# First two modulation items between the turns of x, sum of squares behind them, cached rows ahead of the key items

## The chip, the cores and the metric

The kernel runs on one core of a Trainium2 chip. The metric is the device time of one execution in microseconds (us); lower is better.

## The reference

One decoder layer (DEPTH = 1) is computed for a prompt of 256 tokens and for 8 sequences that each decode one token behind 1024 cached positions, in fp32, with D = 1024. Reduced to what matters here:

```python
mod = silu(c) @ ada_w + ada_b              # 9 rows of c (1 prompt, 8 samples), ada_w 1024 x 6144
sh1, sc1, g1, sh2, sc2, g2 = split(mod, 6)
h = rms_norm(x, norm1_w) * (1 + sc1) + sh1  # needs the first third of mod: sh1, sc1
proj = h @ w_in                             # 1024 x 2824: pool, q, k, v, conv q/k/v, z, b, a
q_a, k_a = rms_norm per head                # block-sparse attention, paged K/V cache for the samples
qkv = silu(short_conv(concat(state_conv, [q_d, k_d, v_d])))   # width 4, 3 cached rows per sample
beta, g = gates from b, a;  o = gated_delta_rule(l2norm(q), l2norm(k), v, g, beta, state)
x = x + g1 * (concat(pool, attention, delta) @ w_out)
x = x + g2 * ((silu(h2 @ w_gate) * (h2 @ w_up)) @ w_down)   # h2 = rms_norm(x) modulated by sh2, sc2
```

`rms_norm` divides by the root of the mean of squares over the 1024 channels of a token.

## The kernel before

The kernel is written engine by engine, with semaphores by hand. Tokens lie in the free dimension: `xT`, `hT` and `proj` are [128 channels, chunks, 264 tokens], 256 prompt tokens and the 8 samples. All weights and all cached pages come through a ring of five slots of 1 MB, filled by SyncE (SP) in the order of the list `stream` (L75 to L114); a slot is filled again when the item five places before it has been read. The stream begins with the eight 1 MB blocks of `ada_w` that make sh1 and sc1. Two blocks make one modulation item: `ada(j)` (L346) multiplies blocks 2j and 2j+1 by the turned silu of c (`cT`), and `ada_turn(j)` (L368) turns the result back after ScalarE has copied it (`ada_rows`, L1530). VectorE adds it up in `mod_reduce(j)` (L948), and `norm_half` (L966) applies it to `hT`.

Before the items TensorE turns x and c (L379 to L388) and the small constant rows (L391), and adds the squares that ScalarE makes of each chunk of x over the channels (`ss1`, L392). ScalarE takes the root of that sum (`roots`, L1547), VectorE its reciprocal and multiplies x with it into `hT` (L945, L946). `keep_awake(b, n)` (L338) issues n matmuls of the identity into bank b, which compute nothing that is used; it waits until the bank is free. At the same time GpSimd (POOL) makes masks (L1792 to L1833) and then issues ten small transfers: cached pool and convolution states, the eight gate columns of `w_in` (`wba`), constants, and two copies of states (L1834 to L1850).

Behind that, the list `ORDER` (L86) sets for all engines alike the order of the steps: each engine walks it and does its own part of a step. W1 is a block of two 128-column groups of `w_in` (`project`, L411). QSUM, QNORM and QR make the query norms and the query rows, which POOL stores and spreads over the partitions (L1859 to L1863) for the key items: K0 to K15 are half-sequences of cached keys, each a product and a reduction on VectorE (`k_item`, L1010). CONV is the short convolution on VectorE (`convolve`, L1119), which needs the projections up to W9 and the cached rows; BA and AB make the gates; DSUM and DNORM the norms of its q and k. CEXT stands for the cached rows. On TensorE it is

```python
def cached_rows():
    pe.wait_ge(sem("cst_in"), 16)
    b = opened("cext", 3)
    ... six transposes of cst
    closed(last, "cext")
    pe.wait_ge(sem("pool_rows"), 1)
    b = opened("pdT8", 3)
    ... two transposes of pd8
    closed(last, "pdT8")
```

`opened(name, b)` waits until the last contents of bank b were read, here until VectorE's part of CEXT (L1098) has copied `cext`. That part copies `cext`, waits for `pdT8` and copies that.

Of the kernel before, what the change touches and what calls it, by code (L numbers as in the profile page):

```python
# [35 lines left out]
def build(nc, x_prompt, x_sample, cache_k, cache_v, state_pool, state_conv, state_delta, page_table,  # L36
# [4 lines left out]
    _, T, D = x_prompt.shape  # L41
# [11 lines left out]
    DC = D // P  # L53
# [18 lines left out]
    IW = SLOT // DC  # L72
# [10 lines left out]

    ORDER = ("W1 W2 QSUM W7 QNORM QR QB0 QB1 K0 W8 K1 K2 W9 CEXT W10 CONV BA AB W3 DSUM QB2 K3 W4 DNORM KSUM K4 GN W5 "  # L86
             "QB3 K5 GC KNORM GBC KR ROWS KK W6 K6 QB4 TI VR L1 K7 KROW W0 K8 M1 VROW L2 QB5 K9 M2 TAILS L3 S K10 M3 A4 "
             "H0 QB6 K11 L4 M4 H1 A5 H2 L5 K12 M5 A6 QB7 H3 K13 H4 L6 K14 M6 POOL H5 UA A7 K15 H6 UB UC H7 UD A8 HE OWN "
             "A9 DMAX DEXP V0 XA V1 XB V2 XC V3 XD V4 MX V5 V6 MW0 V7 VE MD MW1").split()
    ORDER = [(st.rstrip("0123456789"), int("0" + st.lstrip("ABCDEFGHIJKLMNOPQRSTUVWXYZ"))) for st in ORDER]  # L90
    for st, n in ORDER:
        if st == "W":
# [7 lines left out]

    win_order = [n for st, n in ORDER if st == "W"]

# [16 lines left out]
    with ctx:  # L119
# [6 lines left out]
        def sem(name):  # L126
            if name not in sems:
                sems[name] = ctx.enter_context(nc.semaphore(name))
            return sems[name]
# [143 lines left out]

        EARLY = sum(st == "MW" for st, n in ORDER)
        part_free = {}
# [12 lines left out]
        def full(eng, name):  # L288

            b, n = filled[name]  # L290
            eng.wait_ge(bank_full[b], n)
            return bank[b]

        def freed(ins, name):
            ins.then_inc(bank_free[filled[name][0]], 1)
# [24 lines left out]
        def _(pe):  # L320
            def opened(name, b, readers=1):

                if frees[b]:
                    pe.wait_ge(bank_free[b], frees[b])
                fills[b] += 1
                frees[b] += readers
                assert name not in filled, name
                filled[name] = (b, fills[b])
                freed_by[name] = frees[b]
                return bank[b]  # L330

            def closed(ins, name):
                ins.then_inc(bank_full[filled[name][0]], 1)
# [4 lines left out]
            def keep_awake(b, n):  # L338

                if n and frees[b]:  # L340
                    pe.wait_ge(bank_free[b], frees[b])
                for _ in range(n):
                    mm(bank[b][:, 0:P], ident[:, :], ident[:, :])


            def ada(j, b_=3, awake=0):  # L346

                opened(f"ada{j}", b_)
                for n in range(2):
                    keep_awake(1, awake)  # L350
                    last = ada_half(j, n)
                    if n == 0:
                        used_up(last, ("ada", 2 * j), "pe_read")
                closed(last, f"ada{j}")
                read_by(f"ada{j}", ("ada", 2 * j + 1))
# [20 lines left out]
            pe.wait_ge(sem("ident_made"), 1)  # L376
            keep_awake(7, 8)
            pe.wait_ge(sem("x_in"), 16 * (TT + 1))
            for c in range(DC):  # L379
                b = opened(f"xT{c}", 4 + c % 4)  # L380
                for r in range(TT):
                    pe.transpose(b[:, r * P:(r + 1) * P], x_nat[:, r, c * P:(c + 1) * P], ident[:, :])  # L382
                closed(pe.transpose(b[:, T:NT], x_nat[0:NS, TT, c * P:(c + 1) * P], ident[0:NS, 0:NS]), f"xT{c}")
            pe.wait_ge(sem("c_silu"), 1)
            b = opened("cT", 0)
            for c in range(DC):
                last = pe.transpose(b[:, c * NC:(c + 1) * NC], c_nat[:, c * P:(c + 1) * P], ident[32:32 + NC, 32:32 + NC])
            closed(last, "cT")  # L388
            pe.wait_ge(sem("rows_in"), 16 * 11)
            b = opened("rowsT", 1)  # L390
            closed(pe.transpose(b[:, 0:NR], rows[0:NR, :], ident[0:NR, 0:NR]), "rowsT")  # L391
            b = opened("ss1", 6)  # L392
            for c in range(DC):
                pe.wait_ge(sem("sq1"), c + 1)
                last = mm(b[:, 0:NT], ones[:, :], hT[:, c, :], c == 0, c == DC - 1)
            closed(last, "ss1")
            pe.wait_ge(sem("cT_made"), 1)
            ada(0, 2)
            ada(1, 3)
            ada_turn(0, 0)  # L400
            ada(2, 2)
            ada_turn(1, 1)
            keep_awake(0, 4)
            ada(3, 3, 2)
            ada_turn(2, 0)
            keep_awake(1, 3)
            ada_turn(3, 1)
            keep_awake(0, 8)
            pe.wait_ge(sem("masks_made"), 1)
# [390 lines left out]
            }  # L800
            for st, n in ORDER:
                if st in go:
# [28 lines left out]
            for i in range(D // IW):  # L831
                w = parts(("wout", i))
                for n in range(2):
                    j = 2 * i + n
# [77 lines left out]
        def _(v):  # L912
# [16 lines left out]
            for c in range(PCH):  # L929
                for g in range(2):  # L930
                    r = slice(64 * g, 64 * g + 64)
                    step(v.tensor_scalar(rcnt[r, c, :], rcnt[r, c, :], float(WINDOWS[2 * c + g]), None, ALU.min))
            for c in range(DC):
                b = full(v, f"xT{c}")
                freed(v.tensor_copy(xT[:, c, :], b[:, 0:NT]), f"xT{c}")
            b = full(v, "cT")
            freed(v.tensor_copy(cT[:, :, 0:NC], b[:, 0:DC * NC].rearrange("p (c r) -> p c r", c=DC)), "cT")
            v.wait_ge(bank_free[0], frees_at("cT"))
            v.sem_inc(sem("cT_made"), 1)
            b = full(v, "rowsT")  # L940
            freed(v.tensor_copy(constT[:, 0:NR], b[:, 0:NR]), "rowsT")
            v.wait_ge(bank_free[1], frees_at("rowsT"))
# [565 lines left out]
        def _(a):  # L1508
# [29 lines left out]
            def roots(name, banks, scale, done):  # L1538
                for c in range(banks):
                    nm = f"{name}{c}" if banks > 1 else name  # L1540
                    b = full(a, nm)
                    freed(a.activation(rbc[:, c, :], b[:, 0:NT], ACT.Sqrt, bias=eps[:, 0:1], scale=scale), nm)
                    a.wait_ge(bank_free[filled[nm][0]], frees_at(nm))
                    a.sem_inc(sem(done), 1)


            roots("ss1", 1, 1.0 / D, "root1")  # L1547
            for j in range(2 * D // IW // 2):
                ada_rows(j)

            def proj_out(item):
# [385 lines left out]
        @block.sync  # L1937
        def _(sp):
            sp.dma_start(c_nat[0:1, :], c_prompt).then_inc(sem("c_in"), 16)
            sp.dma_start(c_nat[1:NC, :], c_sample).then_inc(sem("c_in"), 16)  # L1940
            cols = {"ada": ada_w, "win": w_in, "wout": w_out, "gate": w_gate, "up": w_up}
            for it in stream:
                kind, i = it
                if it == ("k", (0, 0)):
                    sp.wait_ge(sem("table_in"), 16)
                if kind in "kv":

                    load_pages(sp, it, range(PGI // 2 if kind == "v" and i[0] >= 2 else PGI))
                    continue
                if it in before:  # L1950
                    sp.wait_ge(*released[before[it]])
                s = place[it][0]
                dst = ring[:, s, :]
                if kind == "down":
                    k0, k1 = DKT[i[1]]
                    sp.dma_start(dst[:, 0:(k1 - k0) * IW].rearrange("p (k n) -> p k n", n=IW),
                                 w_down[0, k0 * P:k1 * P].rearrange("(k p) n -> p k n", p=P)[:, :, i[0] * IW:(i[0] + 1) * IW])\
                      .then_inc(slot_full[s], 16)
                else:
                    sp.dma_start(dst.rearrange("p (k n) -> p k n", k=DC),  # L1960
                                 cols[kind][0].rearrange("(k p) n -> p k n", p=P)[:, :, i * IW:(i + 1) * IW])\
                      .then_inc(slot_full[s], 16)
                if it == ("win", 6):

                    sp.wait_ge(sem("sq1"), 1)
                    for c in range(GC):
                        for w in range(2):
                            sp.dma_start(Ss[64 * w:64 * w + 64, :, c, :],
                                         state_delta[0, :, 2 * c + w].rearrange("q k n -> k q n")).then_inc(sem("S_in"), 16)

            rows_at = 0
            for i in range(D // IW):
                cols_i = slice(i * IW, (i + 1) * IW)
                for r in (0, 2, 1) if i == D // IW - 1 else range(TT + 1):
                    if (i, r) == (D // IW - 1, 1):
                        sp.wait_ge(sem("y_last"), 1)
                    else:
                        rows_at += 1
                        sp.wait_ge(sem("y_rows"), rows_at)
                    if r < TT:  # L1980
                        sp.dma_start(y_prompt[0, r * P:(r + 1) * P, cols_i], ynat[:, r, cols_i]).then_inc(sem("y_out"), 16)
                    else:
                        sp.dma_start(y_sample[:, 0, cols_i], ynat[0:NS, TT, cols_i]).then_inc(sem("y_out"), 16)
            sp.wait_ge(sem("y_out"), 16 * (TT + 1) * (D // IW))
# [29 lines left out]
```

## Time and profile before

| what | value |
|---|---|
| median of 3 runs | 596.73 us (593.17 to 600.68) |
| the profiled execution | 596.88 us |
| its span, first to last instruction | 594.9 us |
| TensorE busy | 534.4 us, 90% of the span |
| VectorE busy | 350.0 us, 59% |
| ScalarE busy | 163.5 us, 27% |
| moved by DMA | 116.79 MB, mean 196 GB/s |
| mean granted TensorE clock | 0.947 of full speed |

A busy TensorE counts matmuls from start to modelled end, so its 90% is not 90% of its peak, and keep-awake matmuls are in it. The granted clock has two levels, 1.2 and 2.4 GHz; 1.00 in a row is the higher, 0.50 the lower, and a value between is a mean over the stretch. The chain of work that ended last says which instruction or transfer each next one waited for, back from the end. In a timeline row the bracket gives how long the engine stood idle before and what it waited for.

### The profile page before, as it was taken

To read this page: it belongs to the slowest core of one execution; us is meant where nothing else is said; L and a number is where in the kernel's file an instruction comes from. 1 tells how busy PE (TensorE), PEld (TensorE's weight loads), DVE (VectorE), ACT (ScalarE), POOL (GpSimd) and SP (SyncE) were. 2 spreads that over 40 slices of the span, in tenths; PEclk is the share of its full clock that TensorE was granted. 3 is DMA by queue.
4 is the path that set the end of the run, shared out by engine and by line. 5 is a ranking of instruction groups with operands and counts; after the bars stand their busy time and mean duration, and the time that the engine had idled before them with its cause. 6 is when DMAs were issued, how large, how long until landed. Compare 5 with 4: busy or idle time off the path is not lost.

```text
span 594.9 us, 10233 instructions
## 1 busy us (share of the span) xinstructions
PE 534.4 (90%) x3943; PEld 450.2 (76%) x3943; DVE 350.0 (59%) x548; ACT 163.5 (27%) x230; POOL 56.6 (10%) x126
## 2 busy tenths in 40 slices
PE   7879997997998888988789689987999999999997
PEld 5557775675688766865564059887999999999996
DVE  4540269478798787955734537465665566455441
ACT  4101010811132122211000224364343443424420
POOL 6800010000104800000101000000000000000000
PEclk8979897997699999999969899998999999999999
DMA  9996356476049467643739998595465655645201
GB/s 294 332 302 207 108 189 218 123 204 221 19 150 324 144 221 245 217 132 119 244 111 376 384 352 268 173 298 163 148 209 162 195 169 168 195 144 193 73 19 37
DMA packets 98998, 116.79 MB, mean 196 GB/s; under 512 B 6317, under 2 KB 81278, under 8 KB 98934
## 3 DMA queue, kind: packets, MB, share of 16 engines
q1 hardware_dynamic: 93218, 104.42, 54.8%
q10 hardware_dynamic: 3908, 7.42, 3.5%
q0 software_dynamic: 1824, 4.30, 2.6%
q8 instruction: 31, 0.51, 0.4%
q14 instruction: 17, 0.14, 0.1%
HBM read 113.30 MB, written 2.99 MB: 195 GB/s over the span
## 4 chain that ended last, share of the span: by engine, by line
PE 64%; DVE 21%; DMA 7%; ACT 3%; issue 3%; ACTq 1%; SPq 0%; DVEq 0%
PE bank L336 61%; DVE prod L916 5%; DVE s_all L1019 5%; DVE mats L916 3%; DMA ring<-in_ada_w_dram 2%; DMA ring<-in_w_out_dram 2%; DVE BTP L916 1%; DVE cv L1127 1%; DMA ring<-in_cache_v_dram 1%; DMA x_nat<-in_x_sample_dram 1%; PE bank L373 1%; PE bank L382 1%; ACT w_part L1692 1%; DMA qb<-q_rows_dram 1%; PE bank L517 1%
## 5 line engine op out<-in xcount | busy, mean ns | idle before, releaser
L336 PE MATMUL bank<-a_hi,w_part 128*128 128x264 f32 x832 | 153.5, 286 | 2.1 <-DVE a_lo L1464 2.1
L916 DVE TENSOR_TENSOR w_part<-ring,w_part 128x2048 fp32r<-128x2048 f32 (+1 forms) x38 | 84.9, 2236 | 89.2 <-ACT w_part L1692 89.2
L336 PEld LDWEIGHTS bank<-a_hi,w_part 128*128 128x128 f32 x832 | 129.8, 189 | 2.6 <-issue 2.6
L336 PE MATMUL bank<-a_lo,w_part 128*128 128x264 f32 x416 | 118.4, 285 | 0.0
L1692 ACT ACTIVATE w_part<-ring 128x2048 fp32r<-128x2048 f32 (+1 forms) x38 | 70.9, 1871 | 86.0 <-PE bank L336 75.0
L336 PE MATMUL bank<-hT,ring 128*128 128x264 f32 x352 | 85.7, 406 | 0.8 <-ACT proj L1555 0.8
L336 PEld LDWEIGHTS bank<-hT,ring 128*128 128x128 f32 x352 | 70.0, 201 | 14.9 <-issue 2.4
L336 PEld LDWEIGHTS bank<-a_lo,w_part 128*128 128x128 f32 x416 | 79.0, 190 | 0.1
L336 PE MATMUL bank<-hid_hi,w_part 128*128 128x264 f32 x352 | 64.9, 285 | 0.0
L336 PEld LDWEIGHTS bank<-ident 128*128 128x128 f32 x362 | 48.1, 212 | 10.4 <-issue 5.6
L336 PEld LDWEIGHTS bank<-hid_hi,w_part 128*128 128x128 f32 x352 | 54.5, 188 | 0.1
L336 PE MATMUL bank<-ident 128*128 128x128 f32 x362 | 51.5, 301 | 3.3 <-POOLq L1785 1.9
L336 PE MATMUL bank<-hid_lo,w_part 128*128 128x264 f32 x176 | 49.7, 282 | 0.0
L916 DVE TENSOR_TENSOR prod<-ring,qb 128x2048 f32<-128x2048 f32 x16 | 36.5, 2280 | 7.0 <-DMA qb<-q_rows_dram 6.4
L1019 DVE TENSOR_REDUCE s_all<-prod 128x32 f32<-128x2048 f32 x16 | 36.6, 2286 | 0.5
L1555 ACT ACTIVATE proj<-bank 128x264 f32<-128x264 f32 x22 | 8.6, 390 | 89.5 <-PE bank L336 89.4
L336 PEld LDWEIGHTS bank<-hid_lo,w_part 128*128 128x128 f32 x176 | 33.2, 188 | 0.0
L336 PE MATMUL bank<-ring,cT 128*32 128x256 f32 x384 | 24.3, 393 | 6.0 <-DMA ring<-in_ada_w_dram 6.0
L336 PE MATMUL bank<-mats,BTP 128*128 128x128 f32 x192 | 25.0, 280 | 3.4 <-DVEq L1085 2.9
L336 PEld LDWEIGHTS bank<-mats,BTP 128*128 128x128 f32 x192 | 22.9, 191 | 5.2 <-issue 4.0
L336 PE MATMUL bank<-ring,prod 128*32 128x512 f32 x128 | 18.0, 660 | 6.5 <-DMA ring<-in_cache_v_dram 6.5
L336 PEld LDWEIGHTS bank<-ring,cT 128*32 128x32 f32 x384 | 11.3, 111 | 15.3 <-DMA ring<-in_ada_w_dram 6.9
(326 smaller groups left out, 570.3 us busy)
## 6 DMA issues: line engine op xcount, KB each, us to landing
ring<-in_ada_w_dram SPq DMA_DIRECT2D x24, 1024.0 KB, 7.3
ring<-in_cache_k_dram SPq DMA_DIRECT2D x64, 256.0 KB, 3.6
ring<-in_w_in_dram SPq DMA_DIRECT2D x11, 1024.0 KB, 5.6
ring<-in_w_gate_dram SPq DMA_DIRECT2D x11, 1024.0 KB, 5.3
ring<-in_w_up_dram SPq DMA_DIRECT2D x11, 1024.0 KB, 5.3
ring<-in_cache_v_dram SPq DMA_DIRECT2D x40, 256.0 KB, 4.2
ring<-in_w_down_dram SPq DMA_DIRECT2D x8, 1024.0 KB, 5.1
ring<-in_cache_v_dram ACTq DMA_DIRECT2D x24, 256.0 KB, 5.2
```

What stands on the lines that cost most here:

```text
L336: return pe.matmul(out, lhsT, rhs, start=start, stop=stop, skip_group_check=True)
L373: last = pe.transpose(b[:, n * P:(n + 1) * P], ada_flat(j)[:, n * P:(n + 1) * P], ident[:, :])
L382: pe.transpose(b[:, r * P:(r + 1) * P], x_nat[:, r, c * P:(c + 1) * P], ident[:, :])
L517: last = pe.transpose(b[:, n * P:(n + 1) * P], sm[:, h % 2, n * P:(n + 1) * P], ident[:, :])
L916: return v.tensor_tensor(out, a, b_, op)
L1019: ins = v.tensor_reduce(s_all[:, o:o + PGI * H], prod[:, :].rearrange("p (g d) -> p g d", d=HD), AX, ALU.add)
L1127: v.scalar_tensor_tensor(out=cv[:, c, back:T], in0=proj[:, CV0 + c, 0:T - back], scalar=cw(i, c), in1=cv[:, c, back:T], op0=ALU.mult, op1= ...
L1555: freed(a.activation(proj[:, j, :], b[:, 0:NT], ACT.Copy), f"proj{j}")
L1692: inc(a.activation(w_hi[:, n % PARTS, 0:c], arrived(a, item)[:, 0:c], ACT.Copy), "w_high")
```

## The change

In TensorE's first part, c is turned after four of the eight chunks of x instead of after all. The first modulation item is multiplied right behind the turns, then the constant rows are turned, the second item is multiplied, and the sum of squares follows. Two of four keep-awake matmuls ahead of the fourth item and three between the last two turns are taken out. VectorE takes the turned chunks in the same order, and ScalarE copies the first item ahead of the root. In `ORDER`, CEXT moves from behind W9 to behind QSUM, for all engines. SyncE's wait ahead of the delta states' loads, which overwrite the rows of x, is for all eight squares.

```diff
@@ -83,7 +83,7 @@
 
 
 
-    ORDER = ("W1 W2 QSUM W7 QNORM QR QB0 QB1 K0 W8 K1 K2 W9 CEXT W10 CONV BA AB W3 DSUM QB2 K3 W4 DNORM KSUM K4 GN W5 "
+    ORDER = ("W1 W2 QSUM CEXT W7 QNORM QR QB0 QB1 K0 W8 K1 K2 W9 W10 CONV BA AB W3 DSUM QB2 K3 W4 DNORM KSUM K4 GN W5 "
              "QB3 K5 GC KNORM GBC KR ROWS KK W6 K6 QB4 TI VR L1 K7 KROW W0 K8 M1 VROW L2 QB5 K9 M2 TAILS L3 S K10 M3 A4 "
              "H0 QB6 K11 L4 M4 H1 A5 H2 L5 K12 M5 A6 QB7 H3 K13 H4 L6 K14 M6 POOL H5 UA A7 K15 H6 UB UC H7 UD A8 HE OWN "
              "A9 DMAX DEXP V0 XA V1 XB V2 XC V3 XD V4 MX V5 V6 MW0 V7 VE MD MW1").split()
@@ -376,34 +376,39 @@
             pe.wait_ge(sem("ident_made"), 1)
             keep_awake(7, 8)
             pe.wait_ge(sem("x_in"), 16 * (TT + 1))
-            for c in range(DC):
+            def turn_x(c):
+
                 b = opened(f"xT{c}", 4 + c % 4)
                 for r in range(TT):
                     pe.transpose(b[:, r * P:(r + 1) * P], x_nat[:, r, c * P:(c + 1) * P], ident[:, :])
                 closed(pe.transpose(b[:, T:NT], x_nat[0:NS, TT, c * P:(c + 1) * P], ident[0:NS, 0:NS]), f"xT{c}")
+
+            for c in range(DC // 2):
+                turn_x(c)
             pe.wait_ge(sem("c_silu"), 1)
             b = opened("cT", 0)
             for c in range(DC):
                 last = pe.transpose(b[:, c * NC:(c + 1) * NC], c_nat[:, c * P:(c + 1) * P], ident[32:32 + NC, 32:32 + NC])
             closed(last, "cT")
+            for c in range(DC // 2, DC):
+                turn_x(c)
+            pe.wait_ge(sem("cT_made"), 1)
+            ada(0, 2)
             pe.wait_ge(sem("rows_in"), 16 * 11)
             b = opened("rowsT", 1)
             closed(pe.transpose(b[:, 0:NR], rows[0:NR, :], ident[0:NR, 0:NR]), "rowsT")
+            ada(1, 3)
             b = opened("ss1", 6)
             for c in range(DC):
                 pe.wait_ge(sem("sq1"), c + 1)
                 last = mm(b[:, 0:NT], ones[:, :], hT[:, c, :], c == 0, c == DC - 1)
             closed(last, "ss1")
-            pe.wait_ge(sem("cT_made"), 1)
-            ada(0, 2)
-            ada(1, 3)
             ada_turn(0, 0)
             ada(2, 2)
             ada_turn(1, 1)
-            keep_awake(0, 4)
+            keep_awake(0, 2)
             ada(3, 3, 2)
             ada_turn(2, 0)
-            keep_awake(1, 3)
             ada_turn(3, 1)
             keep_awake(0, 8)
             pe.wait_ge(sem("masks_made"), 1)
@@ -930,13 +935,19 @@
                 for g in range(2):
                     r = slice(64 * g, 64 * g + 64)
                     step(v.tensor_scalar(rcnt[r, c, :], rcnt[r, c, :], float(WINDOWS[2 * c + g]), None, ALU.min))
-            for c in range(DC):
+            def take_x(c):
+
                 b = full(v, f"xT{c}")
                 freed(v.tensor_copy(xT[:, c, :], b[:, 0:NT]), f"xT{c}")
+
+            for c in range(DC // 2):
+                take_x(c)
             b = full(v, "cT")
             freed(v.tensor_copy(cT[:, :, 0:NC], b[:, 0:DC * NC].rearrange("p (c r) -> p c r", c=DC)), "cT")
             v.wait_ge(bank_free[0], frees_at("cT"))
             v.sem_inc(sem("cT_made"), 1)
+            for c in range(DC // 2, DC):
+                take_x(c)
             b = full(v, "rowsT")
             freed(v.tensor_copy(constT[:, 0:NR], b[:, 0:NR]), "rowsT")
             v.wait_ge(bank_free[1], frees_at("rowsT"))
@@ -1544,8 +1555,9 @@
                     a.sem_inc(sem(done), 1)
 
 
+            ada_rows(0)
             roots("ss1", 1, 1.0 / D, "root1")
-            for j in range(2 * D // IW // 2):
+            for j in range(1, 2 * D // IW // 2):
                 ada_rows(j)
 
             def proj_out(item):
@@ -1962,7 +1974,7 @@
                       .then_inc(slot_full[s], 16)
                 if it == ("win", 6):
 
-                    sp.wait_ge(sem("sq1"), 1)
+                    sp.wait_ge(sem("sq1"), DC)
                     for c in range(GC):
                         for w in range(2):
                             sp.dma_start(Ss[64 * w:64 * w + 64, :, c, :],
```

## Rows read from the trace of the kernel before

**Rows 1.** Chain that ended last, first 72 us: start us, us, what.

```profile
22.05 12.68 DMA ring<-in_ada_w_dram
...
37.76 1.28 PE bank L336 x6
...
39.89 16.32 PE bank L336 x80
```

**Rows 2.** Stretches: us, engines' busy us (count), PEclk, DMA share, GB/s.

```profile
8.00:20.00 12.00, 12.00 (x71) 8.38 (x74) 7.83 (x12) 5.59 (x11) 8.92 (x37) 0.72 1.10 348
20.00:22.00 2.00, 2.00 (x44) 1.21 (x40) 1.97 (x2) 0.60 (x1) 1.68 (x6) 1.00 0.80 233
22.00:29.00 7.00, 5.23 (x68) 3.22 (x60) 2.67 (x5) 1.20 (x2) 6.28 (x10) 1.00 1.10 365
29.00:34.00 5.00, 1.53 (x20) 0.78 (x12) 0.00 (x0) 0.00 (x0) 1.92 (x4) 0.95 1.05 172
```

**Rows 3.** Timeline, first 45 us: start, us, engine, line, operation, [idle before].

```profile
7.37 1.06 ACT L1525 ACTIVATE x_nat<-x_nat 9x1024 f32<-9x1024 f32 x1
...
12.65 1.01 PE L387 MATMUL bank<-ident,x_nat 9*128 9x9 f32 x8
...
18.80 3.66 PE L336 MATMUL bank<-ring,cT 128*32 128x256 f32 x64
...
21.31 2.36 DVE L916 TENSOR_TENSOR hT<-xT,rbc 128x2112 f32<-128x2112 f32 x1
21.35 2.41 POOL L1829 TENSOR_SCALAR_AFFINE_SELECT lvl<-lvl 128x64 f32<-128x64 f32 x1
...
24.72 0.57 POOL L1834 DMA_DIRECT2D mats<-in_state_pool_dram  x1 [0.65 <-POOL lvl L1831]
...
37.86 0.60 ACT L1534 ACTIVATE adaS<-bank 128x512 f32<-128x512 f32 x1 [10.02 <-PE bank L373]
```

**Rows 4.** Timeline of SyncE, 19 to 23 us: sixth to eighth block.

```profile
19.93 2.70 SPq L1960 DMA_DIRECT2D ring<-in_ada_w_dram  x3
```

**Rows 5.** Timeline, 59 to 98 us: W7, reciprocal, query norm, CEXT, W10, convolution.

```profile
59.77 7.39 PE L336 MATMUL bank<-hT,ring 128*128 128x264 f32 x32
...
60.42 1.79 DVE L991 RECIPROCAL rbc<-rbc 8x264 f32<-8x264 f32 x1 [14.44 <-ACTq L1597]
...
67.83 0.93 DVE L997 SCALAR_TENSOR_TENSOR proj<-proj,constT,bank 128x264 f32<-128x264 f32 x2 [5.62 <-PE bank L336]
...
92.85 0.31 DVE L1100 COPY cext<-bank 128x144 f32<-128x144 f32 x1
...
93.30 0.35 PE L476 MATMUL bank<-ident,vb 8*128 8x8 f32 x2 [5.42 <-DVE cext L1100]
...
93.58 9.73 PE L336 MATMUL bank<-hT,ring 128*128 128x264 f32 x32
...
93.97 1.69 DVE L1122 TENSOR_SCALAR cv<-proj,constT 128x264 f32<-128x264 f32 x6
```

**Rows 6.** Timeline, 103 to 128 us: gates, W3, squares, DSUM, W4, DNORM.

```profile
103.25 3.73 PE L336 MATMUL bank<-hT,wba 128*4 128x264 f32 x32
...
106.91 7.39 PE L336 MATMUL bank<-hT,ring 128*128 128x264 f32 x32
...
107.74 1.08 ACT L1618 ACTIVATE mats<-cv 128x1056 f32<-128x1056 f32 x1
...
114.23 1.95 PE L336 MATMUL bank<-mats,headsum 128*8 128x264 f32 x8
...
116.94 7.36 PE L336 MATMUL bank<-hT,ring 128*128 128x264 f32 x32 [0.77 <-ACT proj L1555]
...
127.28 1.69 DVE L1154 SCALAR_TENSOR_TENSOR cv<-cv,bank 128x264 f32<-128x264 f32 x4 [1.74 <-PE bank L336]
```

**Rows 7.** Stretches at a lower granted clock; columns as in rows 2.

```profile
71.50:74.80 3.30, 3.30 (x11) 2.62 (x10) 0.68 (x1) 0.00 (x0) 0.52 (x1) 0.55 0.06 15
...
93.30:103.10 9.80, 9.80 (x34) 7.90 (x34) 9.20 (x34) 0.39 (x1) 0.00 (x0) 0.74 0.51 180
```

## Prediction

> **What bounds the kernel.** I read four things in turn: the chain that ended last over the first 72 us, the stretches of that part with their DMA share, the timeline around each moved step, and the granted clock behind each long wait of TensorE. In the chain, TensorE is through with its first work by 22 us and then the chain is one transfer for 12.68 us: the eighth modulation block, the last of `ada_w` that the first norm needs, landing at 34.7 [rows 1]. From 39.89 on it is TensorE's dense work, and behind that TensorE and VectorE alternate, so a shift of the chain at 40 us or at 94 us goes through to the end. I see no later transfer that waits for a fixed time: the value pages too wait for ring slots, which work on the chain frees. In the stretches the reader is to see that the DMA engines are full from 8 us to 34 us except for two microseconds: 348 GB/s, then 233, then 365, then 172 although the share is 1.05 [rows 2].
>
> **The front, and what it can gain.** Turns of x run from 7.5 us. The silu of c ends at 8.43 (7.37 + 1.06), before the fourth turn is over, so `cT` between the turns makes nobody wait; its eight transposes (1.01 us) only change places [rows 3]. The matmuls of `ada(0)` then start at about 13.9 instead of 18.80 (18.80 less the sum of squares, which moves behind). The first block is read by about 15.7, so the sixth to eighth blocks are queued at 15.7 to 19 instead of from 19.93 on [rows 4]. What this buys is only the hole that they left in the queue: (348 - 233) GB/s x 2 us is 230 KB, or 0.7 us at 348 GB/s [rows 2]. Beyond that the blocks cannot come faster than 348 GB/s.
>
> Then comes the stretch from 29 to 34 us at 172 GB/s [rows 2]. It is the one in which POOL's own transfers (cached states, `wba`, `poolw`), issued from 24.72 on, are in flight [rows 3]. POOL gets to them after its masks, and one mask instruction took 2.41 us beside VectorE's 2.36 us product of x and the root, where its neighbours take some 0.24 [rows 3]. That product needs the sum of squares, which now ends near 23.4 (the second item is through near 19.8, when its fourth block has landed; then 16 matmuls, half of W3's 7.39 [rows 6]), so it runs at some 26 to 28 us: POOL issues about 2.2 us earlier, still ahead of the eighth block. So I take it that the slow stretch stays in front of the eighth block, and count 0.7. The ends: 0 if the earlier POOL transfers cost the blocks as much as the hole did, and 0.7 + (348 - 172) / 348 x 5 us = 3.2 if the slow stretch falls behind the block. I take 0.7 because nothing in the rows moves POOL's transfers later.
>
> The Trainium skill, "DMA: Bandwidth & Descriptors", section on queues, rings and completion order, says that a DMA engine goes round between the queues that have work, a packet of each at a time. By it POOL's earlier start takes turns from the blocks, and the front would give nothing; the 172 GB/s agrees, but no row shows the order of the packets.
>
> The later sum of squares costs nothing: before, the product ended 4.9 us after the sum (21.31 + 2.36 less 18.80), so now near 28.3, and the first two reductions by about 29.3, under cover of the eighth block until about 34. If that block landed before 29, they would be next. `keep_awake(0, 2)` waits for bank 0, freed by the first of these reductions at about 28.5; behind it only the seventh block's matmuls are queued, which ran near that time anyway. Of the keep-awake matmuls taken out, those of 1.28 us between the last two turns were on the chain [rows 1], but the last turn also waits for ScalarE's copy (37.86 + 0.60) [rows 3]: I take 0.2, ends 0 and 1.28. SyncE's wait for eight squares instead of one, far into the stream, is fulfilled long before: 0. No DMA changes its place on SyncE's queue, since CEXT loads nothing. Front: 0.9 us earlier.
>
> **CEXT ahead of W7.** On TensorE it opens bank 3 twice; the second opening (`pdT8`) waits until VectorE has copied the first. Where it stands now that copy waits behind three key items, and TensorE waits 5.42 us [rows 5]. That wait is off the chain: the convolution behind it needs W9 only, done before. In its new place VectorE still has the query reciprocal ahead of the copy (60.42 + 1.79 = 62.21). Copy to second transpose is 93.30 - 92.85 = 0.45, and from there to the next weights 93.58 - 93.30 = 0.28 [rows 5]. So W7 starts at 62.98 by the old clock instead of 59.77: 3.2 us late. VectorE hides nothing of it: it stood 5.62 us idle for W7 and the query spread [rows 5]. Queued behind W7 are the spread, the query rows, their two transfers, and K0 to K2: all 3.2 us later. On VectorE the two copies and their handshakes vanish from between K2 and the convolution: 93.97 - 92.85 = 1.1 back [rows 5]. Their new cost lies in VectorE's idle 5.62. Net, the convolution starts 2.1 late.
>
> **What is late next.** With the wait gone, TensorE runs W10 (7.4 at full rate, as W3), the gates (3.73) and W3 (7.39) straight behind W9, and is through with W3 near 108.7 (the old end of W9 at 87.9, + 3.2 - 0.9, and these three) instead of 114.2. Nobody can use this. DSUM needs the squares that ScalarE ends at 107.74 + 1.08 = 108.8 [rows 6], now later by 2.1 - 0.9 = 1.2, so at 110.0; it takes 1.95. W4 needs banks that ScalarE frees after its decay work, at 116.94, now 118.1 [rows 6]. VectorE's decay step no longer waits for the gates, but ScalarE is the late one there: 0. So TensorE stands idle from about 112.0 to 118.1, 6 us where it was 0.77 [rows 6]. The only wait of that length nearby is the 5.42 before W10; there the granted clock went to the lower level, 1.2 GHz, for part of the stretch (mean 0.74), and W10 took 9.73 us against 7.39 for the same work [rows 5 to 7]. W4 I expect to take the same 2.3 us more. This is on the chain: VectorE idles 1.74 for the spread behind W4 [rows 6]. Ends: 0 (clock held) and 7.4 (all of W4 at half rate); I stay at the one row for such a wait.
>
> **The sum.** - 0.9 + 3.2 - 1.1 + 2.3 = +3.5 us on the profiled execution's 596.88 (span 594.9 and 2.0 around it): 600.4. The median shown, 596.73, is 0.15 below that execution, so against it 600.2. The three runs spread over 593.17 to 600.68, so 2% (12 us) is about what can be told from no change, and the forecast is "no change", on the slow side.
>
> **Rivals.** W7 runs at the lower clock too. TensorE now idles some 2.3 us before it. For: after smaller gaps near 70 us the clock went down for 71.5 to 74.8 (mean 0.55), costing 0.45 x 3.3 = 1.5 us [rows 7]. Against: the wait of 0.77 before W4 cost nothing. Sum +5.0: 601.7.
>
> The front gives nothing, by POOL's transfers coming 2.2 us earlier. For: the 172 GB/s. Against: the hole at 20 to 22 us is certain. Only the 0.2 is left: +4.2, 600.9. This is also what the Trainium skill's rule gives.
>
> W4 keeps its clock. Then +1.2: 597.9. Against it stands the only wait of like length.
>
> Faster. The slow stretch falls behind the eighth block: front 3.2 + 0.2, and with all shifted W4 at full rate: -3.4 + 2.1 = -1.3, 595.4. It decides where the eighth block lands before 32 us. Against: POOL issues earlier, not later.
>
> Slower beyond 2%. VectorE's later alternation with TensorE holds key items between steps of the triangular solve at fixed places. If the shift sent TensorE to the lower clock there, as before W10, at 2.3 us each four such places on top of the sum pass 12 us (3.5 + 9.2 = 12.7): 609.4. Nothing in the change moves the order there, so I count it little.
>
> **How the numbers follow.** Chances: forecast 0.38, W7 also slow 0.20, no front gain 0.16, W4 keeps its clock 0.10, faster 0.12, slower beyond 0.04. All but the last lie within 2%: faster 0.01 (a front and a clock better than both ends), same 0.95, slower 0.04. The range goes from the faster case, 595.4, less a little for the spread of the runs, to W7 slow and no front together (+3.5 + 1.5 + 0.7 = +5.7: 602.4), with as much on top for a longer stretch at the lower clock in W4: 595 to 604.
>
> **What would show it.** After: `ada(0)` near 14 us; the hole at 20 to 22 us gone; the eighth block near 34.0; a wait of TensorE for VectorE's `cext` copy of 2 to 2.5 us, now at about 60 to 62 us; K0's product 2.3 us later than before; no wait before W10; TensorE idle about 6 us before W4, and W4 near 9.7 us. I am wrong if the eighth block lands before 32, if W7 starts no later than before, or if W4 takes 7.4.

## The result, and the profile after

The changed kernel takes 602.53 us (median of 12 runs, 601.09 to 609.22), the kernel before, run beside it, 599.23 us (12 runs). The ratio is 1.0087 with a 95% interval of 1.0048 to 1.0126: slower by some 5.2 us (2.9 to 7.5), under 2% but clear of noise. The ratio compares the means of the fast runs (603.7 and 598.5 us, one slow run of the kernel before left out), while the medians lie 3.3 us apart. The profiled execution took 601.52 us with a span of 599.6 us, 4.7 us more than before.

The chain of waits of the changed kernel (start us, us, what; answers to [rows 1]):

```profile
19.84 15.43 DMA ring<-in_ada_w_dram
...
39.75 16.04 PE bank L336 x80
```

Its stretches (columns as in [rows 2]):

```profile
8.00:20.00 12.00, 12.00 (x89) 6.79 (x93) 4.85 (x11) 5.48 (x11) 8.92 (x37) 1.00 1.10 348
20.00:22.00 2.00, 2.00 (x18) 1.38 (x11) 2.00 (x1) 0.61 (x1) 1.43 (x7) 1.00 1.10 349
22.00:26.80 4.80, 4.80 (x49) 3.32 (x48) 2.26 (x2) 1.08 (x2) 4.33 (x8) 1.00 1.14 357
26.80:34.30 7.50, 3.47 (x32) 2.22 (x31) 3.36 (x5) 0.60 (x1) 1.85 (x4) 1.00 1.08 238
```

The reader is to see that the hole at 20 to 22 us is closed (349 GB/s for 233), that the slow stretch has come forward and grown longer, and that the transfer on the chain ends at 35.3 (34.7 before), while x landed 0.5 us later. The 1.00 granted from 8 to 20 us, for 0.72 before, is not to be read as a gain. Two transposes of x take 0.69 us there, as they did before once the clock had fallen (0.50 from 10 to 12 us), and not the 0.44 of the higher clock. The first line is of the changed kernel, the two others of the kernel before:

```profile
8.00 0.69 PE L383 MATMUL bank<-ident,x_nat 128*128 128x128 f32 x2 [2.31 <-DMA x_nat<-in_x_sample_dram]
...
7.49 0.44 PE L382 MATMUL bank<-ident,x_nat 128*128 128x128 f32 x2 [1.79 <-DMA x_nat<-in_x_sample_dram]
...
9.58 0.68 PE L382 MATMUL bank<-ident,x_nat 128*128 128x128 f32 x2
```

Its timeline up to W1 (start us, us, engine, line, operation; answers to [rows 3, 4]):

```profile
9.83 12.58 SPq L1972 DMA_DIRECT2D ring<-in_ada_w_dram  x4
...
15.31 3.23 PE L336 MATMUL bank<-ring,cT 128*32 128x256 f32 x32
...
22.48 0.57 POOL L1846 DMA_DIRECT2D mats<-in_state_pool_dram  x1 [0.65 <-POOL lvl L1843]
...
26.83 2.36 DVE L921 TENSOR_TENSOR hT<-xT,rbc 128x2112 f32<-128x2112 f32 x1
...
35.31 1.94 PE L336 MATMUL bank<-ring,cT 128*32 128x256 f32 x16 [2.74 <-DMA ring<-in_ada_w_dram]
...
39.09 0.66 PE L373 MATMUL bank<-ident,adaS 128*128 128x128 f32 x4 [0.80 <-ACTq L1547]
```

The steps come in the forecast order, and POOL issues 2.24 us earlier (22.48 for 24.72), as forecast. `ada(0)` starts at 15.31 instead of near 14, and the eighth block, at 35.31, is no earlier. The last turn now runs at the higher clock (0.66 us); before, it took 1.06:

```profile
38.83 1.06 PE L373 MATMUL bank<-ident,adaS 128*128 128x128 f32 x4
```

What two queues moved from the start of the span to the landing of the eighth block (packets, MB, share of the 16 engines; q1 is SyncE's queue, q0 POOL's), first before, to 34.73 us, then after, to 35.27 us:

```profile
q1 hardware_dynamic: 8739, 8.84, 85.9%
q0 software_dynamic: 271, 0.28, 4.8%
...
q1 hardware_dynamic: 9016, 9.11, 87.0%
q0 software_dynamic: 384, 0.46, 6.6%
```

After, 0.18 MB more of POOL's transfers and 0.27 MB more of SyncE's queue, that is of the blocks behind the eighth, were moved by the time the eighth had landed.

From QSUM to the convolution (answers to [rows 5]):

```profile
59.99 1.79 DVE L1002 RECIPROCAL rbc<-rbc 8x264 f32<-8x264 f32 x1 [13.47 <-ACTq L1609]
61.71 0.23 DVE L1111 COPY cext<-bank 128x144 f32<-128x144 f32 x1
...
62.09 0.26 PE L481 MATMUL bank<-ident,vb 8*128 8x8 f32 x2 [2.21 <-DVE cext L1111]
...
62.27 9.07 PE L336 MATMUL bank<-hT,ring 128*128 128x264 f32 x32
...
72.10 0.89 DVE L1008 SCALAR_TENSOR_TENSOR proj<-proj,constT,bank 128x264 f32<-128x264 f32 x2 [9.48 <-PE bank L336]
...
90.42 7.39 PE L336 MATMUL bank<-hT,ring 128*128 128x264 f32 x32 [0.43 <-DMA ring<-in_w_in_dram]
...
96.65 1.69 DVE L1133 TENSOR_SCALAR cv<-proj,constT 128x264 f32<-128x264 f32 x6
```

The 5.42 us that TensorE waited for the copy before W10 have become 2.21 before W7; W10 is at full rate (7.39), but W7 takes 9.07 where it took 7.39. The clock behind that wait, as a stretch (answers to [rows 7]):

```profile
62.00:66.00 4.00, 3.91 (x11) 3.15 (x12) 0.17 (x1) 0.00 (x0) 0.00 (x0) 0.57 0.02 4
```

From W3 to DNORM (answers to [rows 6]):

```profile
101.40 7.39 PE L336 MATMUL bank<-hT,ring 128*128 128x264 f32 x32
...
111.54 1.95 PE L336 MATMUL bank<-mats,headsum 128*8 128x264 f32 x8 [2.76 <-ACT mats L1630]
...
119.61 9.43 PE L336 MATMUL bank<-hT,ring 128*128 128x264 f32 x32 [6.12 <-ACT proj L1567]
...
132.01 1.70 DVE L1165 SCALAR_TENSOR_TENSOR cv<-cv,bank 128x264 f32<-128x264 f32 x4 [3.85 <-PE bank L336]
```

TensorE has W3 behind it 5.5 us sooner and then idles 6.12 us before W4, which takes 9.43 for 7.36. The clock at the start of W4, as a stretch:

```profile
119.61:123.50 3.89, 3.89 (x9) 3.06 (x10) 1.59 (x1) 2.11 (x3) 0.00 (x0) 0.50 0.00 0
```

To compare executions whose x lands at different times I take distances in each trace: from the first turn of x to the eighth block's first matmul, from there to W1, and from W1's start to later starts (with the duration in brackets). K4 is the key item behind W4; "rest" is from K4 to the end of the span. The rows below "after" are the experiments of the next section.

| kernel | x to block 8 | block 8 to W1 | W7 | K0 | convolution | W4 | K4 | rest |
|---|---|---|---|---|---|---|---|---|
| before | 27.29 | 7.01 | 17.98 (7.39) | 37.12 | 52.18 | 75.15 (7.36) | 90.90 | 462.2 |
| after | 27.31 | 6.06 | 20.90 (9.07) | 41.34 | 55.28 | 78.24 (9.43) | 96.06 | 462.2 |
| a2_again | 27.89 | 8.10 | 21.26 (8.95) | 41.41 | 55.35 | 78.31 (9.42) | 96.12 | 465.3 |
| e1_front | 27.46 | 8.11 | 18.44 (7.39) | 38.35 | 53.41 | 76.45 (7.36) | 92.19 | 463.5 |
| e2_cext | 29.94 | 4.74 | 20.90 (7.39) | 39.28 | 53.23 | 76.19 (9.73) | 94.30 | 462.6 |
| e3_bank5 | 28.33 | 4.73 | 18.57 (7.39) | 37.31 | 51.25 | 74.20 (9.73) | 92.32 | 464.7 |
| e4_awake | 28.46 | 4.74 | 22.88 (7.39) | 41.49 | 55.43 | 84.33 (7.29) | 100.00 | 464.6 |
| e5_awake_fit | 27.51 | 6.06 | 20.90 (7.39) | 40.51 | 54.46 | 77.76 (7.29) | 93.43 | 462.0 |
| e6_bank5_awake | 28.49 | 8.10 | 19.00 (7.39) | 37.72 | 51.66 | 76.30 (7.29) | 91.97 | 460.3 |
| p1_pool_only | 25.34 | 4.74 | 17.96 (7.39) | 37.20 | 52.26 | 75.22 (7.36) | 90.96 | 462.8 |
| p2_front_pool | 25.20 | 4.74 | 17.97 (7.39) | 37.77 | 52.82 | 75.78 (7.36) | 91.53 | 463.2 |
| p3_all | 24.71 | 4.73 | 18.57 (7.39) | 37.15 | 51.10 | 74.05 (7.36) | 89.80 | 461.1 |
| p4_behind_qr | 24.61 | 4.73 | 17.98 (7.39) | 37.09 | 51.04 | 73.99 (7.36) | 89.73 | 462.7 |
| p5_no_awake | 24.62 | 4.73 | 17.97 (7.39) | 38.03 | 51.97 | 74.93 (9.22) | 92.53 | 462.5 |

So after less before is: W1 0.42 earlier (41.37 for 41.79), W7 2.92 later and 1.68 longer, the way from W7's end to K0 0.38 shorter, from K0 to the convolution 1.12 shorter, W4 2.07 longer, the rest equal: 4.7 us. W1 itself is 0.93 earlier against x, and x landed 0.51 later.

### The profile page after: what moved, and what is told of

Its sections match the earlier page's. It is cut to its first block, busy times and chain, and to the rows that moved or that the text cites. A ratio compares the mean times of both kernels' runs of the same rounds, so it can differ in the third digit from the quotient of the medians.

```text
span 599.6 us, 10213 instructions
## 1 busy us (share of the span) xinstructions
PE 532.8 (89%) x3933; PEld 447.4 (75%) x3933; DVE 349.6 (58%) x548; ACT 163.3 (27%) x230; POOL 54.3 (9%) x126
## 4 chain that ended last, share of the span: by engine, by line
PE 64%; DVE 21%; DMA 7%; ACT 3%; issue 3%; ACTq 1%; DVEq 0%
PE bank L336 60%; DVE prod L921 5%; DVE s_all L1030 5%; DMA ring<-in_ada_w_dram 3%; DVE mats L921 3%; DMA ring<-in_w_out_dram 2%; DVE BTP L921 1%; DVE cv L1138 1%; DMA ring<-in_cache_v_dram 1%; DMA x_nat<-in_x_sample_dram 1%; PE bank L383 1%; PE bank L373 1%; ACT w_part L1704 1%; DMA qb<-q_rows_dram 1%; PE bank L522 0%
## 5 line engine op out<-in xcount | busy, mean ns | idle before, releaser
L336 PEld LDWEIGHTS bank<-ident 128*128 128x128 f32 x352 | 45.7, 208 | 12.5 <-issue 5.1
L336 PE MATMUL bank<-ident 128*128 128x128 f32 x352 | 49.4, 298 | 5.6 <-DVE modT L963 2.3
L336 PE MATMUL bank<-ring,cT 128*32 128x256 f32 x384 | 25.6, 409 | 2.7 <-DMA ring<-in_ada_w_dram 2.7
```

What stands on the lines that cost most here:

```text
L336: return pe.matmul(out, lhsT, rhs, start=start, stop=stop, skip_group_check=True)
```

## Experiments

Each diff is against the changed kernel unless it says otherwise. Where a run has a ratio, it is to the kernel before, run beside it, and need not be the quotient of the two medians; a single profiled execution stands behind each line of the table.

**The front alone.**

```diff
-"W1 W2 QSUM CEXT W7 QNORM ... K2 W9 W10 ..."
+"W1 W2 QSUM W7 QNORM ... K2 W9 CEXT W10 ..."
```

> The changed kernel with CEXT back behind W9, so only the part up to W1. Theory (the whole loss comes from CEXT, the front is a small gain): W1 starts 0.4 to 1 us earlier than before against the landing of x, and the time is 0 to 1 us under the kernel before, ratio 0.998 to 1.000. Within it: the eighth block lands no earlier (27.3 us behind the landing of x, as in both kernels so far), and the gain is the keep-awake matmuls left out. Rival (the sum of squares behind the two items is late and costs): W1 later, ratio above 1.003.

Measured: 0.997 (0.9932 to 1.0007), 597.79 us. The eighth block lies 27.46 us behind x, as expected, so it gains nothing. In the profiled execution, which at 602.41 us was the second longest of twelve, W1 is not earlier: it comes 8.11 us behind the block, at the lower clock, where eleven of the other executions have 4.7 to 7.0 and two have 8.10. A small gain is likely and not shown; a loss as large as the change's is excluded.

**CEXT alone**, in the kernel before.

```diff
-"W1 W2 QSUM W7 QNORM ... K2 W9 CEXT W10 ..."
+"W1 W2 QSUM CEXT W7 QNORM ... K2 W9 W10 ..."
```

> The kernel before with only CEXT moved ahead of W7. Theory: W7 starts 2.5 to 3.2 us late, runs at the lower clock at first (about 1.7 more), the convolution starts about 3.7 late, TensorE idles 6 us before W4 and W4 takes 2 us more; the key item behind it is 5 to 6 us late, ratio 1.009 to 1.011. Rival (the wait is covered, the loss is in the front): ratio 0.998 to 1.002.

Measured: 1.0084 (1.0051 to 1.0117), 603.48 us: as slow as the whole change. The lines of its timeline:

```profile
63.27 0.26 PE L476 MATMUL bank<-ident,vb 8*128 8x8 f32 x2 [2.21 <-DVE cext L1100]
63.45 7.39 PE L336 MATMUL bank<-hT,ring 128*128 128x264 f32 x32
...
118.74 9.73 PE L336 MATMUL bank<-hT,ring 128*128 128x264 f32 x32 [4.84 <-ACT proj L1555]
```

The wait is the same 2.21 us, yet W7 kept the full clock in this execution. K4 lies 3.40 us later against W1 than before (94.30 for 90.90): this is the case that I had forecast as the likeliest, with 4.4 for these terms. My expectation of a slow W7 here was a miss, though this execution (601.40 us) was the fastest of its twelve, and it does not tell how W7 ran in the others.

**CEXT without the wait.**

```diff
-b = opened("pdT8", 3)                        # TensorE
+b = opened("pdT8", 5)
-v.wait_ge(bank_free[3], frees_at("pdT8"))    # VectorE
+v.wait_ge(bank_free[5], frees_at("pdT8"))
```

> The changed kernel with the second transpose group of CEXT (pdT8) in bank 5 instead of bank 3, so that TensorE does not wait for VectorE's copy. Theory: W7 starts 0.5 us behind QSUM's end at the full clock (7.4 us), K0 is on time, the convolution starts about 2 us earlier than before, but TensorE still idles some 6 us before W4, which takes 9.4 us: the two cancel, ratio 0.998 to 1.002. If W4's clock is not on the chain: 2 us faster than before, ratio 0.996. If the wait at W7 is not what costs: as the changed kernel, ratio 1.008.

Measured: 1.0028 (0.9997 to 1.006), 599.11 us; its interval ends below the changed kernel's 1.0087, but overlaps that kernel's interval, which begins at 1.0048. So the time leans to a gain over the changed kernel and does not settle it.

```profile
58.45 0.27 PE L481 MATMUL bank<-ident,vb 8*128 8x8 f32 x2
58.65 7.39 PE L336 MATMUL bank<-hT,ring 128*128 128x264 f32 x32
...
114.28 9.73 PE L336 MATMUL bank<-hT,ring 128*128 128x264 f32 x32 [4.83 <-ACT proj L1567]
```

No wait, W7 0.59 later than before against W1, the convolution 0.93 earlier; and still K4 is 1.42 later, because W4 has the lower clock. The gain of moving CEXT is eaten there.

**Keep-awake matmuls in both waits**, first too many.

```diff
 closed(last, "cext")
+keep_awake(4, 18)          # e5_awake_fit: 9
 ...
+if item == 4:
+    keep_awake(3, 48)      # e5_awake_fit: 22
```

> The changed kernel with keep-awake matmuls in its two new waits: 18 between CEXT's two transpose groups, 48 ahead of W4. The waits stay as long. Theory (wait 2.5 net of the front, W7's clock 1.7, W4's clock 2.1): W7 and W4 at 7.4 us each, the time about 3.8 us under the changed kernel, ratio to the kernel before 1.001 to 1.003. Rival (the clock is off the chain, only the wait counts): as the changed kernel, ratio 1.008.

Measured: 1.0087 (1.0049 to 1.0125), 606.04 us. I had taken 0.12 us for one keep-awake matmul; in the trace it is 0.23 to 0.24:

```profile
113.92 10.98 PE L336 MATMUL bank<-ident 128*128 128x128 f32 x96
124.74 7.29 PE L336 MATMUL bank<-hT,ring 128*128 128x264 f32 x32
```

48 of them (96 instructions) took 11.0 us, so W7 and W4 were pushed later by the filler. The run says nothing on the question, and was repeated with half.

> The changed kernel with keep-awake matmuls that fit its two new waits: 9 (2.2 us at 0.244 each, as the trace shows) between CEXT's transpose groups, 22 (5.4 us) ahead of W4; the run before had twice that and pushed W7 and W4 later itself. Theory (the clock at W7 and W4 is on the chain): W7 and W4 at 7.4 us, W4's start as in the changed kernel, the key item behind it 2 to 4 us nearer to W1 than there (96.06 us behind W1's start), ratio to the kernel before 1.002 to 1.005. Rival (only the wait counts): 96 us behind W1, ratio 1.008.

Measured: 1.0017 (0.9974 to 1.0059), 601.74 us. The interval overlaps the changed kernel's, so the trace has to decide.

```profile
62.23 7.39 PE L336 MATMUL bank<-hT,ring 128*128 128x264 f32 x32
...
114.08 5.18 PE L336 MATMUL bank<-ident 128*128 128x128 f32 x44
119.09 7.29 PE L336 MATMUL bank<-hT,ring 128*128 128x264 f32 x32
```

W7 starts exactly as in the changed kernel against W1 (20.90) and takes 7.39; W4 takes 7.29; K4 is 2.63 nearer to W1 (93.43 for 96.06). That work which computes nothing shortens the way to K4 shows that the clock after the two waits is on the chain. What is left against before is 2.53 us: the wait at W7 (2.92), 0.47 between W7 and K0, where the clock fell somewhat later instead (0.50 from 74 to 76 us), and 0.33 at W4's start, which the fill pushed; off this come 1.11 for the copies taken from VectorE and 0.08 behind W4's start.

**No wait and a filled idle time.** Bank 5 as above, and 22 keep-awake matmuls ahead of W4.

> CEXT ahead of W7 with pdT8 in bank 5 (no wait) and 22 keep-awake matmuls ahead of W4. Theory: W7 0.6 us later than before against W1, the convolution 0.9 earlier, W4 0.9 earlier and at the full clock, so the key item behind it 0.9 earlier against W1 (90.0 instead of 90.9); with the front, ratio 0.995 to 0.998. Rival (W4's clock off the chain): as the run with bank 5 alone, 92.3 behind W1, ratio 1.003.

Measured: 0.9982 (0.9948 to 1.0017), 598.43 us. W4 at 7.29. In this execution the lower clock still held behind W1's start (W1 and W2 took 14.84 for 14.41), and the fill pushed W4 (its keep-awake matmuls took 6.30 us, part of them at the lower clock), so K4 lies at 91.97 and not at 90.0. Against before no more than "not slower" is shown. Against the changed kernel a gain is shown, since the two intervals lie apart: without the wait, and with the idle time filled, the loss is gone.

**POOL's transfers behind the eighth block**, with the front alone and with the kernel before.

```diff
+g.wait_ge(sem("ada_rows"), 4)
 g.dma_start(pbuf, state_pool[0]...)
```

> The front of the change alone (CEXT behind W9) with POOL's ten transfers issued only after ScalarE's fourth copy, that is behind the eighth block. Theory (the front gained nothing at the eighth block because POOL's transfers, earlier by 2.2 us, took the DMA engines that the closed hole gave): the slow stretch moves behind the block, which lands 3 us earlier, some 24.3 us behind the landing of x instead of 27.3, W1 2 to 3 us earlier, ratio 0.991 to 0.995. Rival (the block is late for another reason, as its own queue): 27.3 us, ratio as the front alone, 0.997.

Measured: 0.9889 (0.9845 to 0.9934), 593.51 us. Its stretch from 29 to 34 us, and its timeline:

```profile
29.00:34.00 5.00, 4.58 (x48) 2.82 (x48) 1.01 (x4) 0.00 (x0) 0.00 (x0) 1.00 1.10 349
```

```profile
29.36 1.35 PE L336 MATMUL bank<-ident 128*128 128x128 f32 x8 [2.08 <-DVE modT L963]
30.64 1.07 PE L336 MATMUL bank<-ring,cT 128*32 128x256 f32 x16
31.64 0.71 PE L336 MATMUL bank<-ident 128*128 128x128 f32 x4
32.28 1.07 PE L336 MATMUL bank<-ring,cT 128*32 128x256 f32 x16
```

The stretch that stood at 172 GB/s is at 349. The eighth block's matmuls start 2.1 us earlier behind x (25.20 for 27.29), not the 3 expected, and no longer wait for it: TensorE waits 2.08 us for `modT` ahead of `keep_awake(0, 2)`, which is the late sum of squares coming through VectorE. TensorE no longer stands idle ahead of the block (2.74 us in the changed kernel, 4.25 before), and the clock stays up: block 8 to W1 4.74 for 6.06 and 7.01.

> The kernel before with only POOL's ten transfers issued behind ScalarE's fourth copy (order of the front and CEXT as before). It tells what the hole of 2 us in the DMA engines is worth once nothing else is ahead of the eighth block. Theory (hole 0.7 us, POOL's transfers the rest): the eighth block lands some 26 us behind the landing of x, against 25.2 with the changed front and 27.3 before; ratio 0.990 to 0.994. Rival (the changed front is what lets the late transfers gain): 27.3, ratio 0.998 or more.

Measured: 0.9939 (0.9907 to 0.9971), 592.95 us.

```profile
20.00:22.00 2.00, 2.00 (x40) 1.20 (x40) 1.46 (x1) 0.59 (x2) 1.42 (x7) 1.00 0.45 141
22.00:29.00 7.00, 5.83 (x83) 3.61 (x72) 3.71 (x6) 1.67 (x3) 0.00 (x0) 1.00 1.03 329
29.00:34.00 5.00, 3.70 (x45) 2.15 (x44) 0.00 (x0) 0.00 (x0) 0.00 (x0) 1.00 1.10 349
```

With the old front the block lies 25.34 us behind x, with the hole wide open (141 GB/s). The two fronts differ by 0.14 us here, and by 0.63 to 0.73 against the three runs below, which have the new front too (24.61 to 24.71). Each front has its own brake: the old one the hole, the new one the late sum of squares. What the closed hole is worth by itself stays open.

**All together, and CEXT where VectorE waits anyway.** p3_all: the change with bank 5, 22 keep-awake matmuls ahead of W4 and POOL late. p4_behind_qr: the same with CEXT behind QR. p5_no_awake: that without the keep-awake matmuls.

```diff
-"W1 W2 QSUM CEXT W7 QNORM QR QB0 ..."
+"W1 W2 QSUM W7 QNORM QR CEXT QB0 ..."
```

> All together: the change with pdT8 in bank 5, 22 keep-awake matmuls ahead of W4, and POOL's transfers behind the eighth block. Theory: the gains add, W1 about 24.3 + 5 us behind the landing of x, the key item behind W4 90 us behind W1, ratio 0.988 to 0.993. Rival (late POOL transfers hold up W1's or W2's weights or the cached rows): no faster than the front alone, 0.997.

Measured: 0.9892 (0.9847 to 0.9937), 592.5 us of 6 runs; K4 89.80 behind W1.

> The changed front, POOL's transfers late, CEXT behind QR (where VectorE waits 6 us for the query rows) with pdT8 in bank 5, and 22 keep-awake matmuls ahead of W4. Theory: W7 as before (17.98 us behind W1's start), the convolution 1.1 earlier, W4 1.1 earlier at the full clock, the key item behind W4 some 89.5 to 89.8 us behind W1 (before 90.9); ratio 0.985 to 0.990. Rival: W4's start does not follow the convolution, 90.9.

Measured: 0.9928 (0.9897 to 0.9959), 593.6 us. W7 is as before, the convolution 1.14 and K4 1.17 earlier against W1, as expected; the ratio misses the 0.985 to 0.990.

> As p4_behind_qr without the keep-awake matmuls ahead of W4: TensorE idles some 6 us there. Theory: W4 starts as in p4_behind_qr and takes 9.4 to 9.7 us instead of 7.4, the key item behind it 2.0 to 2.4 us later against W1; ratio 0.989 to 0.994. Rival (the clock at W4 off the chain): no difference.

Measured: 0.9958 (0.9925 to 0.9991), 594.81 us. W4 without the keep-awake matmuls:

```profile
111.42 9.22 PE L336 MATMUL bank<-hT,ring 128*128 128x264 f32 x32 [5.73 <-ACT proj L1567]
```

and with them:

```profile
104.29 5.18 PE L336 MATMUL bank<-ident 128*128 128x128 f32 x44
110.48 7.36 PE L336 MATMUL bank<-hT,ring 128*128 128x264 f32 x32 [1.01 <-ACT proj L1569]
```

The same work costs 1.86 us more behind 5.73 us of idling. K4 is 2.80 later (92.53 for 89.73), more than the 2.0 to 2.4 expected, because W4 did not start as in p4_behind_qr: 0.94 had gone already between W7 and K0, where the clock was down for longer (at 0.50 up to 74 us here, up to 70 us in p4_behind_qr). The two ratios overlap, so the pair shows the price in the trace, and only leans the same way in the time. The five versions with POOL's transfers late beat both kernels; their order among themselves is not told by these intervals.

**The changed kernel once more.**

> The changed kernel once more, for one look at another execution. It tells whether W7's lower clock behind CEXT's wait belongs to the kernel or to the execution: the kernel before with CEXT alone moved had the same wait and W7 at the full clock (7.39 us). If it belongs to the execution, W7 may take 7.39 here and the key item behind W4 lies 94.3 us behind W1 instead of 96.1; if to the kernel, 9.07 and 96.1 again. W4 at the lower clock (9.2 to 9.7 us) in both.

One execution, 606.82 us, beside 595.91 of the kernel before:

```profile
64.83 8.95 PE L336 MATMUL bank<-hT,ring 128*128 128x264 f32 x32
...
121.88 9.42 PE L336 MATMUL bank<-hT,ring 128*128 128x264 f32 x32 [6.12 <-ACT proj L1567]
```

W7 and W4 are slow again, K4 96.12 behind W1. So both profiled executions of the changed kernel have the slow W7, and the one of CEXT alone has not. What decides it is open.

## Why the prediction was wrong, step by step

The time is inside the range and has the forecast's sign, and 3.5 us lies inside the measured 2.9 to 7.5. Two steps failed. One is the call: 3.5 us was put down as "no change", and the kernel is slower clear of noise. The other is the price of CEXT's wait: the sum has W7 at the full clock behind it, a term of 0, and I put the lower clock into a rival at 0.20, with +5.0 us. In the profiled pair this rival is what came: 4.7 us, with W7 1.68 longer, of which 1.30 reached K0. The times alone (3.3 by the medians, 5.2 by the ratio) do not tell +3.5 from +5.0. Of the 1.25 us between the forecast and the profiled pair, W7's clock makes 1.30 and the late x 0.51; the other terms take 0.56 off.

- *Front, the hole (0.7 forecast, 0.0 measured).* The hole closed, and the block came 27.31 us behind x for 27.29. That was the rival with 0.16: POOL's transfers moved 2.24 us forward (22.48 for 24.72), and 0.18 MB more of them were moved ahead of the eighth block's landing, 0.5 us at 348 GB/s. I had no term for the other taker, the 0.27 MB more of the blocks behind the eighth, 0.8 us at that rate. No run separates the two. That POOL's transfers as such hold the block up is shown by moving them away: 2.0 us for the old front, 2.1 for the new, and the nine executions with early transfers (27.29 to 29.94) lie apart from the five with late ones (24.61 to 25.34). The 0.0 itself comes from one pair; the seven executions with the new front and early transfers spread from 27.31 to 28.49. My other end, 3.2, was too far, as with them away the late sum of squares, which I had named as next, then holds the chain. The Trainium skill's rule that I weighed ("DMA: Bandwidth & Descriptors", queues, rings and completion order) forecast that the front gains nothing at the block; the trace agrees, with those two distances, though no run shows the order of the packets.
- *Front, keep-awake matmuls (0.2 forecast, 0.95 measured).* Block 8 to W1 is 6.06 for 7.01: the last turn starts 0.27 sooner behind the block (3.78 for 4.05), and the other 0.68 comes behind that start, where the clock was up earlier. Over the executions this distance is 4.7, 6.1, 7.0 or 8.1 by where the clock stands. With the clock up it is 4.74 for the old front too (e2_cext, p1_pool_only), so there the matmuls taken out are worth nothing. So 0.95 is one draw, and the two errors of the front cancelled by luck. x also landed 0.5 later in this execution.
- *CEXT's wait (3.2 forecast, 2.92 measured).* Right in place and mechanism: behind the query reciprocal, with nothing to hide W7. (In its working, 62.21 + 0.45 + 0.28 is 62.94 and not 62.98, which changes no term.)
- *The copies taken from VectorE (1.1 forecast, 1.12 measured).* Right.
- *W7's clock (0 in the forecast, 1.68 measured; W7's end to K0 is 0.38 shorter, so 1.30 net).* The wrong term. I had the row that told it: small gaps near 70 us had brought the clock down [rows 7], and I weighed one wait of 0.77 us against it. With fitting keep-awake matmuls W7 is back at 7.39. In one execution of CEXT alone it was at 7.39 without them, so the cost does not come every time.
- *W4's clock (2.3 forecast, 2.07 measured).* Right, and shown to be on the chain by e5_awake_fit: a wait taken off TensorE where nobody needed it became 6.12 us of idling further on, with W4 at the lower clock and on the chain.
- *SyncE's longer wait, cT between the turns, the covered sum of squares: 0.* Right in the changed kernel; the sum of squares is at 0 only while POOL's transfers hold the block back.

"No change" itself was a misreading: I took the spread of three single runs for what a comparison can tell, where 12 runs against 12 tell 0.4%.

## What to carry to other kernels

When a stall is moved off an engine, ask what that engine is waiting for next: TensorE ran ahead of ScalarE, idled longer, and paid for it at the lower clock. Where TensorE would wait for a copy only to get its PSUM bank back, give the next result another bank, or put the step where the copying engine idles anyway. A hole in a queue is worth its size only if its bytes go to the transfer that is waited for; here small transfers of another engine and later blocks took them. Issuing the small ones later brought 0.6% in the kernel before and 1.1% together with the changed front, both against the kernel before.

## What the runs showed that I had not expected

- The distance from the eighth block to W1, the same instructions but for a few keep-awake matmuls, takes from 4.73 us (clock up) to 8.1 us. So where the clock has fallen during the waits ahead of the block, up to 3.4 us come on top of the waits.
- POOL's issues of small transfers beside VectorE's product of x and the root (26.83 to 29.19) took no longer: the two that lie wholly beside it took 0.53 and 0.52 us, for 0.54 and 0.52 before, when VectorE stood idle. This is so although a mask instruction of POOL beside the same product had taken 2.41 us for 0.24 [rows 3].
- POOL's small transfers (eleven issues by the trace, not the ten of the text above; 448 KB in all) hold up the 1 MB blocks by 2 us: 172 and 238 GB/s over those stretches for 348.
- Keep-awake matmuls shorten a chain when they fit a wait (2.63 us at K4 in e5_awake_fit) and lengthen it when they don't (3.94 in e4_awake).
